# The beginning of a fused decoder layer: memory transposes moved between the two key tiles of each piece, value weights split by the contraction and loaded ahead of x

## What is computed

```python
proj = jnp.einsum('bsd,dc->bsc', x, w_in)            # 512 x 1024 by 1024 x 7168
y_c = _memory_attention(mq, jnp.einsum('bmd,dw->bmw', mem, w_mem_k),
                            jnp.einsum('bmd,dw->bmw', mem, w_mem_v))
...                                                   # conv branch, HGRN2 branch, gates, merge
x = _layer_norm(ALPHA * x + mixed, ln1_g, ln1_b)
h = jnp.square(jax.nn.relu(jnp.einsum('bsd,df->bsf', x, w_up)))
x = _layer_norm(ALPHA * x + jnp.einsum('bsf,fd->bsd', h, w_down), ln2_g, ln2_b)
```

## Time and profile before

| | |
|---|---|
| time, median of 3 runs | 834.19 us (834.16 to 834.86) |
| profiled execution, first to last instruction | 832.3 us |
| what lies around the span, by the median of the runs | 1.9 us |
| TensorE busy | 818.0 us, 98% |
| VectorE, ScalarE, GpSimd busy | 503.0, 351.7, 32.5 us |

### The profile page before, as it was taken

The page is one execution under the profiler, slowest core; times in us unless marked ns, Lnnn a source line. Parts: engine busy times, 40 slices in busy tenths (PEclk is TensorE's granted clock), DMA queues, the critical chain, the costliest instruction groups (busy, mean ns, idle before and its releaser), DMA issues.

```text
span 832.3 us, 10213 instructions
## 1 busy us (share of the span) xinstructions
PE 818.0 (98%) x4111; PEld 695.3 (84%) x4111; DVE 503.0 (60%) x560; ACT 351.7 (42%) x397; POOL 32.5 (4%) x38
## 2 busy tenths in 40 slices
PE   8999999999999999999999999999999999999994
PEld 7989888899888888888888889888888888888883
DVE  3647745567354424414428685986669666956698
ACT  4549343494434223232225035653545345435532
POOL 1110100000001000000000010000000000000005
PEclk9999999999999999999999999999999999999998
DMA  9641313312122322323723407017201810280002
GB/s 311 196 152 52 102 51 102 101 50 94 57 75 88 118 78 98 101 101 101 302 101 97 156 4 250 1 51 263 92 0 51 298 57 0 64 290 1 0 1 101
DMA packets 68215, 87.52 MB, mean 105 GB/s; under 512 B 1581, under 2 KB 51798, under 8 KB 68182
## 3 DMA queue, kind: packets, MB, share of 16 engines
q1 hardware_dynamic: 68182, 87.06, 31.0%
HBM read 84.96 MB, written 2.10 MB: 105 GB/s over the span
## 4 chain that ended last, share of the span: by engine, by line
PE 94%; DVE 4%; issue 1%; DMA 1%; DVEq 0%; SPq 0%; ACT 0%
PE bank L1358 30%; PE bank L1360 30%; PE bank L1359 30%; DVE two L1222 1%; DMA two<-in_mem_dram 1%; PE bank L1572 0%; PE bank L1522 0%; PE bank L1493 0%; PE bank L1640 0%; PE bank L1385 0%; DVE w_lo L808 0%; DVE two L1250 0%; DVE smx L1228 0%; DVE decay L1228 0%; PE bank L1575 0%
## 5 line engine op out<-in xcount | busy, mean ns | idle before, releaser
L1358 PE MATMUL bank<-x_hi,w_hi 128*128 128x512 f32 (+1 forms) x704 | 268.4, 381 | 0.0
L1359 PE MATMUL bank<-x_lo,w_hi 128*128 128x512 f32 (+1 forms) x704 | 267.2, 380 | 0.0
L1360 PE MATMUL bank<-x_hi,w_lo 128*128 128x512 f32 (+1 forms) x704 | 267.2, 379 | 0.0
L803 DVE TENSOR_TENSOR w_lo<-raw,w_hi 128x2048 fp32r<-128x2048 f32 x40 | 91.4, 2290 | 108.0 <-ACT w_hi L511 107.8
L1360 PEld LDWEIGHTS bank<-x_hi,w_lo 128*128 128x128 f32 x704 | 132.4, 188 | 25.0
L1358 PEld LDWEIGHTS bank<-x_hi,w_hi 128*128 128x128 f32 x704 | 132.4, 188 | 24.6
L1359 PEld LDWEIGHTS bank<-x_lo,w_hi 128*128 128x128 f32 x704 | 132.5, 188 | 24.4
L1358 PE MATMUL bank<-w_hi,y_hi 128*128 128x512 f32 (+1 forms) x320 | 121.4, 379 | 0.0
L1360 PE MATMUL bank<-w_hi,y_lo 128*128 128x512 f32 (+1 forms) x320 | 121.1, 378 | 0.0
L1359 PE MATMUL bank<-w_lo,y_hi 128*128 128x512 f32 (+1 forms) x320 | 121.1, 378 | 0.0
L511 ACT ACTIVATE w_hi<-raw 128x2048 fp32r<-128x2048 f32 x40 | 76.4, 1915 | 41.9 <-PE bank L1360 36.8
(11 more groups left out here) (193 smaller groups left out, 847.2 us busy)
## 6 DMA issues: line engine op xcount, KB each, us to landing
raw<-in_w_in_dram SPq DMA_DIRECT2D x28, 1024.0 KB, 5.0
raw<-in_w_up_dram SPq DMA_DIRECT2D x16, 1024.0 KB, 8.5
small<-in_w_down_dram SPq DMA_DIRECT2D x12, 1024.0 KB, 7.1
raw<-in_w_branch_dram SPq DMA_DIRECT2D x6, 1024.0 KB, 5.0
raw<-in_w_o_dram SPq DMA_DIRECT2D x4, 1024.0 KB, 5.0
raw<-in_w_down_dram SPq DMA_DIRECT2D x4, 1024.0 KB, 4.7
two<-in_x_dram SPq DMA_DIRECT2D x2, 1024.0 KB, 11.9
small<-in_w_mem_v_dram SPq DMA_DIRECT2D x2, 1024.0 KB, 12.5
```

What stands on the lines that cost most here:

```text
L803: dve.tensor_tensor(w_lo[:, slot, :], raw[:, r, :], w_hi[:, slot, :].bitcast(F32), ALU.subtract)\
L1358: pe.matmul(dst, a[0], b[0], start=first, stop=False, skip_group_check=goes_on)
L1359: pe.matmul(dst, a[0], b[1], start=False, stop=False, skip_group_check=goes_on)
L1360: return pe.matmul(dst, a[1], b[0], start=False, stop=last, skip_group_check=goes_on)
```

## The change

It does four things.

1. The value weights are loaded as four pieces of 256 rows of the contraction by all 512 columns (512 KB each, `value_landed0` to `3`): two ahead of both halves of x, two behind them. Before, they were two loads of all 1024 rows by 256 columns, one behind each half of x. ScalarE and VectorE convert them in four steps of 1024 elements per partition where there were two of 2048.
2. The value tiles are two of 512 columns (banks 0 and 1) where they were four of 256: 48 products of 512 columns for 96 of 256. The first half of the contraction follows the first 16 transposes of x, the second half the other 16. Each tile is copied out in two halves once both halves of the contraction are in.
3. In the key pieces the transposes of piece j + 1 stand between tile 0 and tile 1 of piece j; before, they stood ahead of both. `keep_busy(8)` and `keep_busy(4)` go, and `keep_busy(10)` comes behind the first transposes.
4. Key tiles 2 and 3 are made by halves of the contraction, with the same 48 products. ScalarE copies key tiles 0 and 1 before it rounds the first value weights, and rounds slab 5 behind the copies of the value tiles.

```diff
             for e in range(2):
-                x_load(e)
-                sp.dma_start(raw_v[:, e].rearrange("p (k c) -> p k c", k=KD), wmv[:, :, e * 256:(e + 1) * 256])\
-                    .then_inc(value_landed[e], 16)
+                for n in range(2 * e, 2 * e + 2):
+                    part = slice(2 * (n % 2), 2 * (n % 2) + 2)
+                    sp.dma_start(raw_v[:, e].rearrange("p (k c) -> p k c", k=KD // 2)[:, part],
+                                 wmv[:, 2 * n:2 * n + 2, :]).then_inc(value_landed[n], 16)
+                if e == 0:
+                    x_load(0)
+                    x_load(1)
...
+            def key_copied(t):
+                act.activation(mem_k[:, t, :], main_of(act, 0, t)[:, 0:M], ACT.Copy).then_inc(main_read[t], 1)
+
+            key_copied(0)
+            key_copied(1)
             value_hi(0)
-            for s in range(4):
-                if s == 2:
-                    x_parts(range(0, 4))
-                    value_hi(1)
-                    x_parts(range(4, KD))
-                    hi(4, 0, 2)
-                elif s == 3:
-                    hi(5, 1, 4)
...
+            key_copied(2)
+            key_copied(3)
+            x_parts(range(0, 4))
+            value_hi(1)
+            x_parts(range(4, KD))
+            hi(4, 0, 2)
+            for c in range(2):
+                act.wait_ge(tile_done, 4 + 2 * (c + 1))
+                for e in (1, 0):
+                    part = slice((1 - e) * 256, (2 - e) * 256)
+                    act.activation(mem_v[:, c, part], bank[c][:, part], ACT.Copy).then_inc(main_read[2 * e + c], 1)
+            hi(5, 1, 4)
...
             keep_busy(10)
             mem_transposed(0)
+            keep_busy(10)
             for j in range(4):
-                if j < 3:
-                    mem_transposed(j + 1)
-                if j < 2:
-                    keep_busy(8 - 4 * j)
                 aux_copied(pe, PRO, "t%d" % j)
...
+                    if c == 0 and j < 3:
+                        mem_transposed(j + 1)
...
+            for e in range(2):
+                pe.wait_ge(x_landed[e], 16)
+                x_transposed(range(4 * e, 4 * e + 4))
+                for c in range(2):
+                    t = bank[c] if e else begin(0, 4 + c)
+                    for k in range(4):
+                        if c == 0 and k == 0:
+                            pe.wait_ge(front_lo, 4 + e + 1)
+                        if c == 0 and k == 2:
+                            slab(2 + e)
+                        mm = three(t, both(memt_hi, memt_lo, ALL, 4 * e + k, slice(c * P, (c + 1) * P)),
+                                   w_part(2 + e, k * WID, WID), e == 0 and k == 0, e == 1 and k == 3)
+                    if e:
+                        mm.then_inc(tile_done, 2)
```

More of the change, by code:

```diff
@@ L238, in build @@
         front_landed = [sem("front_landed%d" % j) for j in range(6)]
-        value_landed = [sem("value_landed0"), sem("value_landed1")]
+        value_landed = [sem("value_landed%d" % n) for n in range(4)]
         x_landed = [sem("x_landed0"), sem("x_landed1")]
@@ L528, in value_hi @@
             def value_hi(e):
-                act.wait_ge(value_landed[e], 16)
-                act.activation(w_hi[:, 2 + e, :], raw_v[:, e], ACT.Copy).then_inc(slab_hi, 1)
+                for n in range(2 * e, 2 * e + 2):
+                    part = slice((n % 2) * SLAB // 2, (n % 2 + 1) * SLAB // 2)
+                    act.wait_ge(value_landed[n], 16)
+                    act.activation(w_hi[:, 2 + e, part], raw_v[:, e, part], ACT.Copy)\
+                        .then_inc(slab_hi if n % 2 else front_hi, 1)
             def x_parts(ks):
@@ L826, in value_lo @@
             def value_lo(e):
-                dve.wait_ge(slab_hi, 2 + e + 1)
-                low_of(w_lo[:, 2 + e, :], raw_v[:, e], w_hi[:, 2 + e, :]).then_inc(slab_lo, 1)
+                for n in range(2 * e, 2 * e + 2):
+                    part = slice((n % 2) * SLAB // 2, (n % 2 + 1) * SLAB // 2)
+                    if n % 2:
+                        dve.wait_ge(slab_hi, 2 + e + 1)
+                    else:
+                        dve.wait_ge(front_hi, 4 + e + 1)
+                    low_of(w_lo[:, 2 + e, part], raw_v[:, e, part], w_hi[:, 2 + e, part])\
+                        .then_inc(slab_lo if n % 2 else front_lo, 1)
             def x_parts(ks):
@@ L1413, in _ @@
                         mm.then_inc(tile_done, 1)
[L1414 to L1429, removed]
-                for c in range(2):
[L1431 to L1438, removed]
+                    if c == 0 and j < 3:
+                        mem_transposed(j + 1)
@@ new lines, in _ @@
+            for h in range(2):
+                if h == 0:
+                    pe.wait_ge(front_lo, 4)
+                else:
+                    slab(1)
+                for c in range(2):
+                    t = (bank[2 + c] if h else begin(0, 2 + c))[:, 0:M]
+                    for k in range(4 * h, 4 * h + 4):
+                        mm = three(t, w_part(1, k * 256 + c * P, P), both(memt_hi, memt_lo, ALL, k),
+                                   k == 0, k == KD - 1)
+                    if h:
+                        mm.then_inc(tile_done, 1)
```

## The result

The change takes 834.91 us (median of 20 runs, 834.55 to 835.51) against 833.94 us (20 runs, 832.26 to 834.86): ratio 1.0014, 95% interval 1.0008 to 1.0020. A ratio is not the quotient of the two medians. The profiled span went from 832.3 to 832.9 us.

What follows compares the result with a forecast made beforehand. TensorE was taken as the bound, busy 818.0 of 832.3 us. Key pieces +1.34 us and value tiles −0.64 us gave +0.7 on the 834.19 us median: 834.9 us, range 833.8 to 836.8 us.

Steps and rivals of the forecast that it cites:

- What bounds: Whole run: TensorE's stream before 16.3 us moves the end one for one; behind that only its length counts.
- The key pieces: Front: piece 0 starts 1.9 us earlier, but three hand-overs stall about 1.5 us each; net +1.34 us.
- my three bounds: Front, by when the clock is fast (6.88, 7.5 or 10.9 us): piece 3 later by 1.08, 1.34 or 2.1 us.
- The clock: Front: TensorE working without pause from 1.54 us reaches its fast pace near 7.5 us, where before about 10.9 us.
- the rival of the late rise: Front: transposes don't raise the clock, products must run about 2 us; +1.5 to +2.5 us in total; chance 0.20.
- the lag of 4.6 us: Front: time from TensorE resuming work at 6.34 us to its fast pace at 10.9 us in the earlier trace.
- Stalls and the clock: Rival, key-piece hand-overs: three 1.5 us gaps keep the clock low or bring it down; 836 to 840 us; chance 0.10.
- Value tiles: Value products: 48 of 512 columns take 10.88 us for 96 of 256 at 11.52 us; −0.64 us, bounds 0.6 and 0.7.
- Covers: After piece 3: loads, value-weight conversions, slab 4 and slab 5 all stay hidden behind TensorE's work; no cost.
- The spare time of slab 4: Before the projections: slab 4's 6.83 us chain just fits TensorE's 7.3 us of work; cover 0.3 us.
- Sum: Whole kernel: +1.34 − 0.64 = +0.7 us, giving 834.9 us, span 833.0 us.

Runs made afterwards that it cites:

- e10: The kernel before, unchanged, profiled a second time: 833.52 us (one run).
- e11: The kernel before, unchanged, profiled a third time: 833.58 us (one run).
- e9: The kernel before without its twelve fillers ahead of pieces 0 and 1: 832.70 us, ratio 0.9987 to the kernel before.
- e5: The change with the next piece's transposes ahead of both key tiles, ten fillers kept: 831.15 us, ratio 0.9970 to the kernel before.
- e4: The kernel before with fourteen more fillers behind the first transposes, in the wait for the second memory piece: 832.81 us, ratio 0.9994.
- e3: The change without the ten fillers behind the first transposes: 836.03 us, ratio 1.0031 to the kernel before.
- e1: The kernel before with only the new order of the key pieces and its ten fillers: 835.53 us, ratio 1.0021.
- e8: The change with the old load order, half of x ahead of each pair of value pieces: 834.93 us, ratio 1.0012 to the kernel before.
- e12: e6 with the old load order, half of x ahead of each pair of value pieces: 830.24 us, ratio 0.9952 to the kernel before.
- e2: The change with the key pieces ordered as in the kernel before, new value tiles and loads kept: 832.95 us, ratio 0.9995.
- e6: The change with eight fillers, second transposes ahead of piece 0, those of piece j + 2 between piece j's tiles: 830.36 us, ratio 0.9961.
- e7: e6 with both remaining transpose sets in piece 0, behind tile 0 and tile 1: 830.46 us, ratio 0.9961 to the kernel before.

## Why the prediction came out as it did

- **What bounds.** Right: the time moved by what the start of TensorE's stream moved and by its length.
- **The key pieces.** Mechanism right, size a little off. Chain 2.70 us (forecast 2.70), piece 3.49 us (3.49), piece 0 at 6.89 us (6.88), each stall 1.55 us from start to start (about 1.5). Piece 3 came at 17.37 us, not 17.61, since the clock had risen before piece 0: +1.10 us for +1.34, the first of my three bounds (1.08). Against the other two profiles of the kernel before it is +1.7. The term was worked out against one execution whose rise was late, and no bound took in that the old front moves too.
- **The clock.** An early rise was forecast, near 7.5 us; the pace doubled near 5 us: ten fillers from 4.58 us took 1.48 us, where eight took 1.91 in the earlier trace rows, and the first products at 6.89 us already step at 0.12. Fast fillers end sooner, hence the fourth wait, 0.83 us ahead of piece 0, which was not forecast and costs nothing, since piece 0 waits for VectorE. Up to then TensorE had run transposes alone. The Trainium skill, TensorE: Matmul & The Clock Gate, Part 4 on the PE-mode transpose, has transposes not counting for the gate; by this row the trace disagrees, and the rival of the late rise falls in the change. The same page, Part 1 on the clock gate, says that the window is free-running and the point of the rise varies by ±0.5 us from run to run. That it varies, e10 and e11 confirm; the size does not agree, with 9.3, 9.7 and 10.9 us in three executions of one program. The reading that the unbroken work from 1.54 to 4.8 us "did not bring" the rise was true of that one execution: e9 had the same work behind it and was fast at 6.76 us. So the lag of 4.6 us, from which 7.5 us was taken, came from a single late rise, and the forecast of an early one was right for a reason that the runs bear out only as a tendency (last section).
- **Stalls and the clock.** Three stalls of 1.39 us left the pace at 0.12 us a product; that rival fell.
- **Value tiles.** −0.56 us for −0.64, below the lower bound of 0.6. The second block of 24 products took 5.62 us (33.55 to 39.17), 0.18 above 24 × 0.2267 for its first product and the turn to the small transpose, where the same two edges cost the kernel before 0.16. The missing part lies mostly in the first block: 5.58 us (26.30 to 31.88) are 0.14 above its pace, where the first block of before (25.21 to 28.16) lay 0.07 above its own. Half of that is a step of about 0.230 us up to 29.15 us, whose cause isn't known.
- **Covers.** All held. The spare time of slab 4 was 0.6 us, or 0.5 with the 0.14 us from VectorE's end to TensorE's start that the forecast of 0.3 had taken off. Its chain took the forecast 6.83 us (31.88 to 38.71); TensorE's side took 7.47, not 7.3.
- **Sum.** +0.7 us forecast, +0.54 us between the two profiled executions, +0.97 us (0.08% to 0.20%) in the runs. The last step, 0.43 us, is no mechanism of the change: the profiled execution of before (834.19 us) lay 0.25 us above its median, that of the change (834.71 us) 0.20 us below. That the forecast of 834.9 us met the median of 834.91 is luck: the front was sized 0.24 us too high, the value tiles' gain 0.08 us too high, and the 0.16 us left between these two were made up by the change's median, 0.20 us above its profiled execution. The part that is not luck is the chain and its cover, 2.70 and 3.49 us, which e5 tried by itself.
- **The spread.** The 20 times of the kernel before lie over 2.6 us, those of the change over 1.0. That the fillers in the wait narrow it is what e4 shows (1.0 us for 3.3 us beside it), and it fits e3 (834.93 to 837.12 us without them).

## What to carry to other kernels

When an engine hands work to others and gets it back, the loss is the length of that chain minus what the engine can do meanwhile: issue the hand-over ahead of all the work that can cover it, not in the middle. Starting the first piece 1.9 us earlier was more than lost while each later hand-over was covered by half as much. Where the first microseconds of TensorE matter, one profile is one draw of the clock's rise; take the profile of the old kernel two or three times before working a sum of a microsecond against it. Work without meaning in an early pause of TensorE made the time of this kernel steadier (e4), at some cost where it kept real work waiting.

## What the runs showed of the hardware

- The rise of TensorE's clock in the same program came at 9.3, 9.7 and 10.9 us; in the change near 5 us, with only transposes run until then; in e3 between 10.6 and 11.8 us. After pauses of 1.88 us (e9) the pace was fast, after 2.10 us (e3) slow.
- Over the fourteen profiles there is a tendency. In the eight where TensorE worked on with fillers behind the first transposes (the change, e1, e4 to e8, e12), the pace had doubled before these fillers ended, between 5.8 and 7.3 us, and before any matrix product. In the six that paused there, it doubled at 9.3 us or later in five (before three times, e2, e3) and before 6.76 us in one (e9). Every kernel but the one before gave one profile, and what decides it in one execution stays open.
- The column of the granted clock reads 1.00 in the stretches ahead of the rise as well; there only the step from product to product (0.21 or 0.12 us for 256 columns) tells the two levels, 1.2 and 2.4 GHz, apart.
- Each stall of 1.4 us left the fast pace as it was (the change, e1, e8).
- From the start of four transposes to the product that needs the low part made from them are 2.70 or 2.71 us at the fast pace, in eleven of the fourteen profiles; in the other three (e6, e7, e12) no product waited for it.
